# A modulation block in the even attentions: half a group behind each of four units, and its row copied behind the exponentials

## The reference

```python
cond = jax.nn.silu(c)
for l in range(DEPTH):
    mod = cond @ ada_w[l] + ada_b[l]          # ada_w: (2, 1024, 6144)
    sh1, sc1, g1, sh2, sc2, g2 = [m[:, None, :] for m in jnp.split(mod, 6, axis=-1)]
    h = _rms_norm(x, norm_mix[l]) * (1.0 + sc1) + sh1
    y = _even_mixer(...) if l % 2 == 0 else _odd_mixer(...)
    x = x + g1 * (y @ w_out[l])
    h = _rms_norm(x, norm_ffn[l]) * (1.0 + sc2) + sh2
    x = x + g2 * _swiglu(h, ...)
```

## Time and profile before

| | |
|---|---|
| median of 3 runs | 2852.78 us (2847.57 to 2852.8) |
| profiled execution | 2850.15 us, span of the profile 2848.4 us |
| TensorE busy | 2680.5 us, 94% of the span |
| VectorE, ScalarE, GpSimd busy | 1153.3, 1072.5, 1236.2 us |
| granted TensorE clock, mean | 0.964 |
| bytes moved by DMA | 265.16 MB, mean 93 GB/s |

### The profile page before, as it was taken

The page is one execution under the profiler, slowest core; times in us unless marked ns, Lnnn a source line. Parts: engine busy times, 40 slices in busy tenths (PEclk is TensorE's granted clock), DMA queues, the critical chain, the costliest instruction groups (busy, mean ns, idle before and its releaser), DMA issues.

```text
span 2848.4 us, 34416 instructions
## 1 busy us (share of the span) xinstructions
PE 2680.5 (94%) x13133; PEld 2139.0 (75%) x13133; DVE 1153.3 (40%) x1794; ACT 1072.5 (38%) x1721; POOL 1236.2 (43%) x652
## 2 busy tenths in 40 slices
PE   6997889999998899999999999999999996999998
PEld 5775567888876578888788888788888662788886
DVE  3168743222137542221226665233321497433312
ACT  3332643332237633332345555233322322433321
POOL 2322533444434244444345555344444484444442
PEclk8998989999999899999999999999999997999998
DMA  9654512223321023223221221223223210232331
GB/s 278 211 169 141 176 31 88 88 91 108 96 74 45 31 75 103 88 92 103 78 74 60 75 60 60 89 89 103 88 96 96 74 59 15 70 107 88 99 97 56
DMA packets 275967, 265.16 MB, mean 93 GB/s; under 512 B 20268, under 2 KB 274829, under 8 KB 275853
## 3 DMA queue, kind: packets, MB, share of 16 engines
q1 hardware_dynamic: 275853, 263.59, 29.4%
HBM read 261.47 MB, written 2.10 MB: 93 GB/s over the span
## 4 chain that ended last, share of the span: by engine, by line
PE 81%; DVE 12%; ACT 3%; issue 2%; SPq 1%; POOL 0%; DMA 0%; DVEq 0%; ACTq 0%
PE bank L1253 20%; PE bank L1254 20%; PE bank L1255 20%; DVE bank L2401 3%; PE bank L985 1%; PE bank L1277 1%; PE bank L987 1%; PE bank L986 1%; PE bank L1279 1%; PE bank L1278 1%; PE bank L976 1%; PE bank L978 1%; PE bank L977 1%; PE bank L1007 1%; PE bank L1357 1%
## 5 line engine op out<-in xcount | busy, mean ns | idle before, releaser
L849 POOL TENSOR_TENSOR w_lo<-w_raw,w_hi 128x1024 fp32r<-128x1024 f32 (+1 forms) x364 | 864.2, 2384 | 1278.0 <-ACT w_hi L1903 744.1
L1253 PE MATMUL bank<-h_hi,w_hi 128*128 128x512 f32 x1632 | 643.9, 395 | 19.2 <-DVE h_lo L2557 12.4
L1254 PE MATMUL bank<-h_lo,w_hi 128*128 128x512 f32 x1632 | 639.6, 392 | 0.0
L1255 PE MATMUL bank<-h_hi,w_lo 128*128 128x512 f32 x1632 | 639.0, 392 | 0.0
L1903 ACT ACTIVATE w_hi<-w_raw 128x1024 fp32r<-128x1024 f32 (+1 forms) x232 | 233.3, 1019 | 481.6 <-PE bank L1255 436.7
L1253 PEld LDWEIGHTS bank<-h_hi,w_hi 128*128 128x128 f32 x1632 | 309.4, 190 | 88.8 <-issue 19.5
L1254 PEld LDWEIGHTS bank<-h_lo,w_hi 128*128 128x128 f32 x1632 | 309.4, 190 | 65.8 <-issue 1.7
L1255 PEld LDWEIGHTS bank<-h_hi,w_lo 128*128 128x128 f32 x1632 | 309.2, 189 | 64.8
L1253 PE MATMUL bank<-a_hi,w_hi 128*128 128x512 f32 x704 | 273.9, 389 | 0.0
L1254 PE MATMUL bank<-a_lo,w_hi 128*128 128x512 f32 x704 | 273.9, 389 | 0.0
L1255 PE MATMUL bank<-a_hi,w_lo 128*128 128x512 f32 x704 | 273.9, 389 | 0.0
(11 more groups left out here) (383 smaller groups left out, 4362.7 us busy)
## 6 DMA issues: line engine op xcount, KB each, us to landing
ada_w<-in_ada_w_dram SPq DMA_DIRECT2D x96, 512.0 KB, 6.2
w_raw<-in_ffn_gate_dram SPq DMA_DIRECT2D x22, 1024.0 KB, 5.2
w_raw<-in_ffn_up_dram SPq DMA_DIRECT2D x22, 1024.0 KB, 5.3
w_raw<-in_ffn_w_gate_dram SPq DMA_DIRECT2D x22, 1024.0 KB, 5.3
w_raw<-in_ffn_w_up_dram SPq DMA_DIRECT2D x22, 1024.0 KB, 5.3
w_raw<-in_ffn_down_dram SPq DMA_DIRECT2D x16, 1024.0 KB, 5.1
w_raw<-in_ssm_w_in_dram SPq DMA_DIRECT2D x16, 1024.0 KB, 5.3
w_raw<-in_ffn_w_down_dram SPq DMA_DIRECT2D x16, 1024.0 KB, 5.1
```

Source lines behind the costliest of these rows:

```text
L849: pool.tensor_tensor(w_lo[parity][:, 0:nk, half], w_raw[parity][:, 0:nk, half], w_hi[parity][:, 0:nk, half].bitcast(F32), ALU.subtract).th ...
L1253: pe.matmul(dst[m][:], hi, src_hi(k0 + k), start=first and k == 0, stop=False)
L1254: pe.matmul(dst[m][:], hi, src_lo(k0 + k), start=False, stop=False)
L1255: ins = pe.matmul(dst[m][:], lo, src_hi(k0 + k), start=False, stop=last and k == nk - 1)
```

## The change

A block of the modulation now takes four steps instead of three. TensorE ends each of steps 0 to 31 with half a group. ScalarE copies the row in the fourth step of a block (`s % 4 == 3`), and does it behind `exps(s)`, not ahead of it. The columns are again the first work of TensorE's next step, `s % 4 == 0`, up to step 32. No instruction is added or taken away.

```diff
 # TensorE
                 for s in range(ATT_STEPS):
-                    if s % 3 == 0 and s // 3 <= ADA_BLOCKS - ADA_PROJ:
-                        ada_columns(ADA_PROJ + s // 3 - 1)
+                    if s % 4 == 0 and s // 4 <= ADA_BLOCKS - ADA_PROJ:
+                        ada_columns(ADA_PROJ + s // 4 - 1)
                     if s < N_UNITS:
                         scores(s)
...
-                    if s % 3 < 2 and s // 3 < ADA_BLOCKS - ADA_PROJ:
-                        for half in range(2):
-                            ada_rows(2 * (ADA_PROJ + s // 3) + s % 3, half)
+                    if s // 4 < ADA_BLOCKS - ADA_PROJ:
+                        ada_rows(2 * (ADA_PROJ + s // 4) + s % 4 // 2, s % 2)
 # ScalarE
                 for s in range(ATT_STEPS):
                     if LAG <= s < N_UNITS + LAG:
                         turned_copy(s - LAG)
-                    if s % 3 == 0 and s // 3 <= ADA_BLOCKS - ADA_PROJ:
-                        ada_take(ADA_PROJ + s // 3 - 1)
-                    if s % 3 == 2 and s // 3 < ADA_BLOCKS - ADA_PROJ:
-                        ada_copy(ADA_PROJ + s // 3)
+                    if s % 4 == 0 and s // 4 <= ADA_BLOCKS - ADA_PROJ:
+                        ada_take(ADA_PROJ + s // 4 - 1)
                     if s < N_UNITS:
                         exps(s)
+                    if s % 4 == 3 and s // 4 < ADA_BLOCKS - ADA_PROJ:
+                        ada_copy(ADA_PROJ + s // 4)
```

## The result

| kernel | median us (lowest to highest) | ratio to the kernel before, 95% interval |
|---|---|---|
| before, beside the first runs | 2852.79 (2847.57 to 2854.0), 4 runs | |
| changed | 2875.89 (2875.16 to 2876.33), 4 runs | 1.0078 (1.006 to 1.0097) |
| changed, measured again | 2876.18 (2875.62 to 2884.29), 6 runs | 1.0077 (1.006 to 1.0094) |

The change makes the kernel 22 us slower, with an interval of 17 to 28. Forecast were +12.6 and 2865.4 us; the time lies inside the range given, 1.1 us under its upper end, and at the price of the first rival, the clock. One execution of the kernel with the columns behind the scores took 4856.9 us at a mean clock of 0.76 and is left out of all that follows, which is why that kernel has two sets of runs.

A forecast was written before the change was run, and what follows sets the result against it. No engine is full: the attention stage is bounded by waits among four in-order queues. Added idle 12.9, less 2.2, plus 1.9 for the clock gave +12.6 us, 2865.4 us; range +8 to +18, eight in ten 2856 to 2877.

The forecast's parts named there:

- the first rival: Attention stage: gaps of 3 to 4 us per block keep TensorE's clock low, say 0.68; +22, 2875 us; chance 0.15.
- (b): Row copy behind exponentials: TensorE's one-step lead is gone, columns wait once per block; 17.7 us over units 7 to 31.
- (c): VectorE falls behind within a group of four, bias starts later; adds 1.0, 1.0 and 0.6 us at units 11, 15, 19.
- The estimates behind the sparse values: Columns' waits after units 27 and 31, where ScalarE's turned copy first waits for sparse values: 1.5 and 0.9 us.
- The longest 3 to 4.5: Sign of being right: TensorE's longest column waits for `ada_row`, 3 to 4.5 us, in the wide units.
- 22 to 24 us: Sign of being right: TensorE's waits at the columns for `ada_row` in the stage, summed over 8 waits.
- 5.14 + 1.0: Unit 15, width 512: bias, exponentials and copy chain of 5.14 us, plus 1.0 for bias starting late on VectorE.
- -2.2 + 1.9: Attention stage clock: slow TensorE work shortens waits, -2.2 us; clock 0.80 instead of 0.83 adds 3.9, half left, +1.9.
- (a): Half row groups spread behind units 0 to 31: 5.5 us of TensorE work leaves steps 3 to 23; no gain counted.
- (d): SP's queue: `w_out` loads issued later, but 30 us or more remain before they are first rounded; cost 0.
- Rival 2: Attention stage: new waits only replace others, stage grows 0 to 5 us, taken 2.5, to 2855 us; chance 0.15.
- Rival 3: Faster: lighter steps 3 to 23 and filled holes behind unit 24, -5.5 us, 2847 us; chance 0.08.

The follow-up runs named there:

- the kernel with repeats: Changed kernel with TensorE doing the next unit's score matmuls 2 to 5 times over ahead of the columns of seven blocks; 2867.53 us, again 2867.82 us.
- the repeated execution: The changed kernel, unchanged, run once more on one chip beside the kernel with repeats; 2876.18 us, ratio 1.0077.

## Why the prediction was right, and where it was off

**The direction and the mechanism (b) were right.** The lead of one unit was given up, and the chain of bias, exponentials and copy stood open on TensorE once per block. That the measured time is inside the range is owed to its width: the sum missed by 10 us, through the term below. The eight waits, predicted with (c) at full clock and then measured after units 3, 7, 11, 15, 19, 23, 27 and 31:

| after unit | 3 | 7 | 11 | 15 | 19 | 23 | 27 | 31 |
|---|---|---|---|---|---|---|---|---|
| predicted | 3.5 | 2.5 | 4.1 | 4.3 | 3.3 | 3.7 | 1.5 | 0.9 |
| measured | 1.62 | 2.78 | 4.15 | 4.56 | 3.32 | 3.75 | 1.30 | 0.88 |

The estimates behind the sparse values held. "The longest 3 to 4.5" and "22 to 24 us" came as 4.56 and 22.4. Only the first wait was clearly too large, by 1.9: the scores of unit 3 no longer wait, half a group fills in, and TensorE was slow there, so its own work (half a group 1.08 us) covered more.

In the wide units the waits came right with both of their terms too small. After unit 15 the chain from the end of the scores (318.19) to the columns (325.64) is 7.5 us, where 5.14 + 1.0 was said, because VectorE began the bias 1.8 us late (319.96) and its part took 3.4 us, not 2.9. What TensorE covers of it is 2.9 us, where 1.8 was said, and 1.0 of that is a new wait for GpSimd's `prob`. After units 7 and 11 it is the same: chains 0.9 and 1.2 us too short, cover 0.6 and 1.1 too small. That the errors cancel to 0.3 us or less is luck.

**The term that failed is the clock.** It stood in the sum as -2.2 + 1.9 = -0.3, on a granted clock of 0.80; measured were 0.73 and 13.2 us more of TensorE's busy time. Two steps were wrong. The first, "where it is low, TensorE's own work between scores and columns lasts twice as long and shortens the wait": the gaps come at the end of an undisturbed stretch, where the clock is up again (0.64 for the half group at 320.44), so nothing was shortened at the four units for which the -2.2 was reckoned. The second, that half of a lower clock is absorbed by waits: the slow matmuls are not spread over the stage. They begin right behind each gap with the columns and the next scores, which are the only work on the chain there and cost 0.8 + 0.95 us at a unit of 512 keys. By the kernel with repeats the low clock costs 12.4 us in the stage. The conversion itself held: busy time x clock, 86.9 us in the kernel before, is 86.1 in the changed one, and with it a clock of 0.73 gives 14.3 us of added busy time (13.2 measured), unhalved. The taken clock of 0.80 and the halving are what failed. Right would have been to ask at which place the clock is low instead of taking the stage's mean.

In the sum: added idle 11.0 (forecast 12.9 less 2.2 = 10.7), added busy time 13.2 (forecast 1.9), together 24.2 in the stage against 12.6. The 10.7 is near 11.0 because the first wait was too large by about what the -2.2 took off wrongly. The first rival had the lower clock at the gaps and its price (+22), the price by two errors that cancel: it took a clock of 0.68 and halved what that costs, and measured were 0.73 and nothing absorbed. Its sign, a stage clock under 0.72, was for the same reason not met (0.73, and 0.75 in the repeated execution), though its mechanism was at work. Its chance of 0.15 was too small, since the evidence for it was in the rows: the lower clock right behind the two gaps of 4.6 and 2.5 us, while the stretch at full clock idled 2.2 us in all.

The Trainium skill ("TensorE: Matmul & The Clock Gate", HAM oscillation) names the pattern of idle gaps between bursts, each followed by work at half rate. The first trace agrees: the five waits of 2.78 to 4.56 us after units 7 to 23 are all followed by columns of 1.86 or 1.87 us. The repeated execution agrees in four of the five, and has the columns behind the 2.78 us at 1.05.

**(a)** held: no gain from the spread (ratio 1.0004). The waits at the end of the stage fell by 2.7 us and others of 3.1 came up elsewhere. **(c)** was right as a mechanism and too small: VectorE's lag is 1.8 us at units 11 and 15, where 1.0 was added, and 0.7 at unit 19 (0.6). **(d)** held: the loads of `w_out` are issued at 387.25 and first rounded at 425.89, 39 us later, where 30 or more had been said.

**Rival 2** is excluded by the starved time of VectorE, 56.3 against 33.3 us. **Rival 3** named what decides, a new wait not above the old one; behind the first it was 3.0 us on average against 1.2. Its source of gain, the spread, gave nothing in any kernel; what gained was another edit, the columns moved in the kernel before.

## What to carry to other kernels

Look how much other work stands in both queues between the producer of a hand-over and its consumer. Here the copy lost one step of lead by a move of one place, and the chain in between came onto TensorE at a cost of 22 to 28 us; moving the consumer one place back (columns behind the next unit's scores) gained 12. Price a gap on TensorE together with the matmuls behind it, at the lower clock, wherever these are what others wait for, and don't halve it. Spreading small work more evenly gained nothing here, where the engines wait for each other in turn.

## What the runs showed of the hardware that was not expected

- Repeating matmuls whose results are thrown away made the kernel 8 us faster (2876.2 to 2867.8 us), with 22 more pairs of scores in the stage and a clock of 0.86 instead of 0.75.
- The clock was up again some 6 us after the end of three of the gaps (columns at 325.64 at 1.86 us, and the half group at 331.66 at 0.64), but only some 12 to 13 us after that of unit 19 (a half group at 356.51 still took 1.08). Behind the waits of 1.30 and 0.88 us (units 27 and 31) it didn't fall for the columns (1.05 us); behind the first of these it fell for the scores (0.80 at 389.05).
- One and the same gap can be followed by either level: 2.78 us after unit 7, with columns of 1.87 us in one execution and 1.05 in another.
- A stage that is 10 us shorter does not always shorten the run by 10: the same kernel had runs at 2837 to 2847 and at 2851 to 2852 us, and in the slower ones that were profiled the rest of the program had 13 us more of TensorE busy time with the same instructions.
